# Shifting the overlaid buffers of a two-layer decoder kernel by 384 bytes per partition

## The chip, the cores and the metric

The kernel runs on one core of a Trainium2 chip. The metric is the device time of one launch in microseconds (us), as the median of three runs. All data are 32-bit floats. Matrix products are done in the fp32r form of TensorE.

## What is computed

The reference is a trunk of two layers on 512 tokens of 1024 channels:

```python
for l in range(DEPTH):                                   # DEPTH = 2
    h = h + hybrid_mixer(rms_norm(h, norm1_g[l]), ...)   # three attention branches, gates, output projection
    h = h + peer_ffn(rms_norm(h, norm2_g[l]), ...)       # 8 heads, top 16 of 16384 experts
return rms_norm(h, final_g)

# the end of hybrid_mixer
merged = (gates[:, :, 0] * (oa @ w_br_a) + gates[:, :, 1] * (ob @ w_br_b) + gates[:, :, 2] * (oc @ w_br_c))
return merged @ w_out

# peer_ffn, per chunk of tokens
act = jnp.einsum('thkd,td->thk', u[ids], xc)
w = g * jax.nn.gelu(act, approximate=False)
y = jnp.einsum('thk,thkd->td', w, v[ids])
```

## The kernel before, in words

**Weights.** Every weight is streamed from HBM in chunks of 128 partitions x 2048 floats (1 MB). SyncE's queue loads a chunk into `raw` (L379). ScalarE copies it to `hi` in the shorter fp32r form (L501), and VectorE writes `lo = raw - hi` (L836). All three have two buffers. Each mathematical product is three matmuls, written by one helper, `product` (L1322):

```python
pe.matmul(dst, a_[0], b_[0], start=first, stop=False)        # L1325  a_hi, b_hi
pe.matmul(dst, a_[0], b_[1], start=False, stop=False)        # L1326  a_hi, b_lo
return pe.matmul(dst, a_[1], b_[0], start=False, stop=last)  # L1327  a_lo, b_hi
```

The first operand of a matmul is the stationary one (128 columns, loaded into the array), the second is the moving one (streamed through it, up to 512 columns). The trace names the moving operand first: `bank<-oT_hi,hi` has `oT_hi` moving and `hi` stationary.

**Stages of a layer, in order of time.** (1) Projections and attention for three pairs of heads. ScalarE and VectorE write the attention output to `oT_hi` and `oT_lo`. (2) Merge: 24 steps M. A step makes the gate product (24 matmuls, `xT` moving, weights stationary, 512 columns) and the branch product (9 matmuls, `oT` moving, weights stationary, 512 columns); in the first four steps of a layer the gate products were done earlier, and the 36 branch matmuls stand by themselves. The merged result goes to `mg_hi` and `mg_lo`. (3) Output projection: 192 matmuls, here `mg` is stationary and the weight chunk moves, 512 columns. (4) Queries and key scores: `xT` moving. (5) U: 64 chunks of 48 matmuls, `xT` moving (352 of the 512 tokens), weights stationary; beside the first 14 the experts are chosen, and beside the next 30 TensorE makes small products of `onehot` tables, which give the gates per expert. (6) V: 64 chunks of 48 matmuls, the weights stationary, `w_hi`/`w_lo` (activation times gate) moving, 352 columns. The other 160 tokens do not go through TensorE in U and V: GpSimd gathers their expert rows by indirect DMA into `rows` (L490), and VectorE multiplies and adds them (L1202 to L1215).

In a V chunk the matmuls run in groups of six: three with `w_hi[:, s, 0]`/`w_lo[:, s, 0]` moving, then three with `w_hi[:, s, 1]`/`w_lo[:, s, 1]`, where `s` is the parity of the chunk.

**How the buffers lie.** SBUF tensors are laid out one after another, in the order of their declarations in `build` (L215 to L306). Sets that are never alive together share one place: `oT`, the attention buffers or the merge buffers, and, over the same bytes, the buffers of the expert stages. Starts in bytes per partition, worked out from the sizes:

| buffer | start before | modulo 1024 | start after | modulo 1024 |
|---|---|---|---|---|
| xT_hi, xT_lo | 32896, 49280 | 128 | same | 128 |
| raw, hi, lo (two each) | 65664 to 106624 | 128 | same | 128 |
| ident | 114816 | 128 | same | 128 |
| keysT | 122496 | 640 | same | 640 |
| oT_hi, oT_lo | 128768, 147200 | 768 | 129152, 147584 | 128 |
| proj | 165632 | 768 | 166016 | 128 |
| v_ab, kv, qT, kT, lg, pT | 180224 to 219136 | 0 | 180608 to 219520 | 384 |
| mg_hi, mg_lo, gates, acc, part, xs | 165632 to 206592 | 768 | 166016 to 206976 | 128 |
| act_s | 133376 | 256 | 133760 | 640 |
| qhT | 145664 | 256 | 146048 | 640 |
| gate_s, onehot, rows | 145664, 178432, 194816 | 256 | 146048, 178816, 195200 | 640 |
| gate_in, w_lo, act_in | 145664, 168192, 179456 | 256 | 146048, 168576, 179840 | 640 |
| w_hi, act_k | 173824, 185088 | 768 | 174208, 185472 | 128 |

A piece of a weight chunk or of `mg` (128 columns) is 512 bytes long, one of `xT`, `oT` 2048, one of `w_hi` 1408.

Of the kernel before, what the change touches and what calls it, by code (L numbers as in the profile page):

```python
# [28 lines left out]
P = 128  # L29
# [177 lines left out]
def build(nc, a, out):  # L207
# [4 lines left out]
    with ExitStack() as ctx:  # L212
        def sb(name, shape, dt=F32, to=ctx):
            return to.enter_context(nc.sbuf_tensor(name, shape, dt))
# [26 lines left out]
        ss, rms, rstd = sb("ss", [P, NT]), sb("rms", [P, NT]), sb("rstd", [P, NT])  # L241
        mx, nmx = sb("mx", [P, NU]), sb("nmx", [P, NU])
        den, esink, rden = sb("den", [P, NU]), sb("esink", [P, NU]), sb("rden", [P, NU])
        to_line = sb("to_line", [P, 8])


        mixer = ExitStack()
# [1561 lines left out]
```

## Time and profile before

| | |
|---|---|
| median of three runs | 3311.99 us (3311.56 to 3313.68) |
| the profiled execution | 3316.17 us, its span 3314.4 us |
| TensorE busy | 3269.3 us, 99% of the span |
| VectorE, ScalarE, GpSimd busy | 79%, 47%, 33% |
| DMA | 894.83 MB, mean 270 GB/s |
| mean granted TensorE clock | 0.998 |

A busy TensorE is not one at its peak: the records of successive matmuls overlap, so the pace is read from the distance of their starts.

### The profile page before, as it was taken

What the parts mean: (1) busy time and instruction counts of PE and PEld (TensorE: products, weight loads), DVE (VectorE), ACT (ScalarE), POOL (GpSimd) and SP (SyncE); (2) the same over time, 40 slices, a digit from 0 to 9 for tenths busy, and PEclk for the clock granted to TensorE, in tenths of its full rate; (3) what the DMA queues carried; (4) which work ended last, traced back from release to release, by engine and by line L of the source; (5) the groups of instructions that cost most, each with busy time, mean ns of one, the idle gap of its engine ahead of it and who ended that gap; (6) DMA issues with size and microseconds to landing.
All of it is one profiled execution on the core that took longest, in us unless ns stands there. A gap on an engine that the chain in (4) does not pass through costs nothing. (4 is left out here: it accounts for less than half of the span.)

```text
span 3314.4 us, 55810 instructions
## 1 busy us (share of the span) xinstructions
PE 3269.3 (99%) x19734; PEld 3039.2 (92%) x19734; DVE 2610.5 (79%) x4992; ACT 1554.9 (47%) x2368; POOL 1087.6 (33%) x711
## 2 busy tenths in 40 slices
PE   8999999999999999999999999999999999999998
PEld 7767878999999999999987678789999999999998
DVE  6555448999997899999855644399999978999897
ACT  5554332467774333333355543334677733333333
POOL 1000003423335555555300000134333345555552
PEclk9999999999999999999999999999999999999999
DMA  4113322479999999999721133224899999999996
GB/s 146 62 52 115 140 104 81 171 286 383 379 383 389 420 403 411 403 409 410 284 90 64 42 124 140 103 82 176 310 379 382 378 404 416 402 409 407 404 405 251
DMA packets 230935, 894.83 MB, mean 270 GB/s; under 512 B 22784, under 2 KB 67984, under 8 KB 182912
## 3 DMA queue, kind: packets, MB, share of 16 engines
q1 hardware_dynamic: 116944, 465.34, 36.7%
q0 software_dynamic: 93008, 337.91, 26.1%
q10 hardware_dynamic: 20832, 89.74, 6.7%
q8 instruction: 72, 1.18, 0.1%
q14 instruction: 79, 0.65, 0.1%
HBM read 801.42 MB, written 91.49 MB: 269 GB/s over the span
## 5 line engine op out<-in xcount | busy, mean ns | idle before, releaser
L836 DVE TENSOR_TENSOR lo<-raw,hi 128x2048 fp32r<-128x2048 f32 (+1 forms) x320 | 728.9, 2278 | 287.4 <-ACT hi L501 284.9
L1325 PE MATMUL bank<-xT_hi,hi 128*128 128x352 f32 (+1 forms) x2688 | 928.7, 346 | 1.9 <-DVE xT_lo L886 1.7
L1326 PE MATMUL bank<-xT_lo,hi 128*128 128x352 f32 (+1 forms) x2688 | 911.5, 339 | 0.0
L1327 PE MATMUL bank<-xT_hi,lo 128*128 128x352 f32 (+1 forms) x2688 | 911.3, 339 | 0.0
L501 ACT ACTIVATE hi<-raw 128x2048 fp32r<-128x2048 f32 (+1 forms) x338 | 643.9, 1905 | 375.9 <-PE bank L1327 338.2
L1325 PE MATMUL bank<-w_hi,hi 128*128 128x352 f32 x2048 | 661.1, 323 | 0.5 <-DVE w_lo L1243 0.5
L1327 PE MATMUL bank<-w_hi,lo 128*128 128x352 f32 x2048 | 661.5, 323 | 0.0
L1326 PE MATMUL bank<-w_lo,hi 128*128 128x352 f32 x2048 | 658.1, 321 | 0.0
L1325 PEld LDWEIGHTS bank<-xT_hi,hi 128*128 128x128 f32 x2688 | 506.5, 188 | 32.3 <-issue 5.6
L490 POOL DMA_INDIRECT rows<-in_v_rows,ids x256 | 415.8, 1624 | 350.5 <-DVE h L1215 276.1
L1327 PEld LDWEIGHTS bank<-xT_hi,lo 128*128 128x128 f32 x2688 | 505.7, 188 | 26.0
L1326 PEld LDWEIGHTS bank<-xT_lo,hi 128*128 128x128 f32 x2688 | 507.2, 189 | 23.1
L490 POOL DMA_INDIRECT rows<-in_u_rows,ids x256 | 325.3, 1271 | 394.0 <-DVE act_row L1204 309.8
L1327 PEld LDWEIGHTS bank<-w_hi,lo 128*128 128x128 f32 x2048 | 386.7, 189 | 0.0
L1325 PEld LDWEIGHTS bank<-w_hi,hi 128*128 128x128 f32 x2048 | 384.4, 188 | 1.6 <-issue 1.0
L1326 PEld LDWEIGHTS bank<-w_lo,hi 128*128 128x128 f32 x2048 | 385.8, 188 | 0.0
L1215 DVE SCALAR_TENSOR_TENSOR h<-rows,w_row,h 128x1024 f32<-128x1024 f32 x256 | 327.6, 1280 | 7.3 <-DVE h L1215 1.4
L1204 DVE CUSTOM_DVE_ANT_0 rows<-rows,x_row 128x1024 f32<-128x1024 f32 x256 | 301.1, 1220 | 12.6 <-DMA rows<-in_u_rows,ids 12.6
L791 ACT ACTIVATE w_hi<-act_in 128x704 fp32r<-128x704 f32 x120 | 95.3, 794 | 392.2 <-DVE act_in L1238 392.2
L706 ACT ACTIVATE act_s<-bank 128x352 f32<-128x352 f32 x124 | 57.6, 465 | 278.3 <-PE bank L1327 278.3
L1262 DVE TENSOR_SCALAR onehot<-iota_sb,idx1T,gT 128x128 f32<-128x128 f32 x704 | 185.8, 356 | 1.0 <-ACT gT L738 1.0
L1623 PE MATMUL bank<-onehot 128*128 128x128 f32 x1408 | 176.0, 275 | 0.0
(227 smaller groups left out, 4254.1 us busy)
## 6 DMA issues: line engine op xcount, KB each, us to landing
raw<-in_stream SPq DMA_DIRECT2D x352, 1024.0 KB, 6.6
gate_d<-gate_s ACTq DMA_DIRECT2D x22, 2048.0 KB, 11.9
act_d<-act_s ACTq DMA_DIRECT2D x120, 352.0 KB, 6.4
act_in<-act_d SPq DMA_DIRECT2D x120, 352.0 KB, 7.0
gate_in<-gate_d SPq DMA_DIRECT2D x96, 384.0 KB, 9.6
gate_in<-gate_d SPq DMA_DIRECT2D x32, 256.0 KB, 4.8
rows<-in_u_rows,ids POOLq DMA_INDIRECT x256, 10.0
rows<-in_v_rows,ids POOLq DMA_INDIRECT x256, 7.5
```

Source lines behind the costliest of these rows:

```text
L490: pool.indirect_dma_start(rows[:, N % NR], None, a["u_rows" if n < U_ROW_OPS else "v_rows"], bass.IndirectOffsetOnAxis(which, 0)).then_inc ...
L501: act.activation(hi[s][:, 0:n], raw[s][:, 0:n], ACT.Copy).then_inc(hi_done, 1)
L706: act.activation(dst[:, s, 1, 0:TU], ps[1][:, 0:TU], ACT.Gelu).then_inc(gelu1, 1)
L791: act.activation(w_hi[:, s], acts_of(k, s), ACT.Copy).then_inc(w_hi_done, 1)
L836: dve.tensor_tensor(lo[s][:, 0:n], raw[s][:, 0:n], hi[s][:, 0:n].bitcast(F32), ALU.subtract).then_inc(lo_done, 1)
L1204: last = dve.tensor_tensor_reduce(row, row, x_row[:], 1.0, 0.0, ALU.mult, ALU.add, act_row[:, k])
L1215: last = dve.scalar_tensor_tensor(out=h[:, ROWED], in0=row, scalar=w_row[:, k], in1=h[:, ROWED], op0=ALU.mult, op1=ALU.add)
L1262: last = dve.tensor_scalar(o[:, r, 0], iota[:], idx1T[:, t], gT[:, t], ALU.is_equal, ALU.mult)
L1325: pe.matmul(dst, a_[0], b_[0], start=first, stop=False)
L1326: pe.matmul(dst, a_[0], b_[1], start=False, stop=False)
L1327: return pe.matmul(dst, a_[1], b_[0], start=False, stop=last)
L1623: last = pe.matmul(ps[4 + slot][:, tile(r)], o[:, 1], o[:, 0], start=True, stop=True)
```

## The change

`to_line` is a tensor that nothing reads or writes. It stands last before the overlaid buffers and grows by 96 floats, 384 bytes. Everything declared before it keeps its place, everything after it (from `oT_hi` on) moves up by 384 bytes. The last buffer then ends at 227968 of 229344. No instruction is added, removed or moved on any engine.

```diff
@@ -241,7 +241,7 @@
         ss, rms, rstd = sb("ss", [P, NT]), sb("rms", [P, NT]), sb("rstd", [P, NT])
         mx, nmx = sb("mx", [P, NU]), sb("nmx", [P, NU])
         den, esink, rden = sb("den", [P, NU]), sb("esink", [P, NU]), sb("rden", [P, NU])
-        to_line = sb("to_line", [P, 8])
+        to_line = sb("to_line", [P, 8 + 96])
```

## Rows read from the trace of the kernel before

**Rows 1.** The page: engines, then 40 slices of the span in tenths.

```profile
PE 3269.3 (99%) x19734; PEld 3039.2 (92%) x19734; DVE 2610.5 (79%) x4992; ACT 1554.9 (47%) x2368; POOL 1087.6 (33%) x711
...
PEclk9999999999999999999999999999999999999999
DMA  4113322479999999999721133224899999999996
```

**Rows 2.** Timeline of PE, one merge step: start us, duration us, engine, line, operands.

```profile
332.94 0.40 PE L1325 MATMUL bank<-oT_hi,hi 128*128 128x512 f32 x1
...
335.04 0.39 PE L1325 MATMUL bank<-xT_hi,hi 128*128 128x512 f32 x1
...
336.42 0.39 PE L1325 MATMUL bank<-xT_hi,hi 128*128 128x512 f32 x1
...
340.50 0.40 PE L1325 MATMUL bank<-oT_hi,hi 128*128 128x512 f32 x1
```

**Rows 3.** Timeline of PE, output projection: its first matmul and what follows its last.

```profile
433.31 0.39 PE L1325 MATMUL bank<-hi,mg_hi 128*128 128x512 f32 x1
...
477.92 0.71 PE L1353 MATMUL bank<-ident_sb,xs 128*128 128x128 f32 x5
```

**Rows 4.** Groups by form, 295 to 433.3 us: count, busy us, mean ns, idle before.

```profile
L1326 PE MATMUL bank<-xT_lo,hi 128*128 128x512 f32 x145 | 56.6, 391 | 0.0
...
L1325 PE MATMUL bank<-oT_hi,hi 128*128 128x512 f32 x57 | 22.5, 395 | 0.0
```

**Rows 5.** Timeline of PE: starts of two successive chunks each, U then V.

```profile
624.50 0.33 PE L1325 MATMUL bank<-xT_hi,hi 128*128 128x352 f32 x1
...
632.24 0.33 PE L1325 MATMUL bank<-xT_hi,hi 128*128 128x352 f32 x1
...
1050.26 0.32 PE L1325 MATMUL bank<-xT_hi,hi 128*128 128x352 f32 x1
...
1057.94 0.32 PE L1325 MATMUL bank<-xT_hi,hi 128*128 128x352 f32 x1
...
2960.28 0.32 PE L1325 MATMUL bank<-w_hi,hi 128*128 128x352 f32 x1
...
2967.91 0.32 PE L1325 MATMUL bank<-w_hi,hi 128*128 128x352 f32 x1
...
3113.86 0.33 PE L1325 MATMUL bank<-w_hi,hi 128*128 128x352 f32 x1
...
3121.59 0.33 PE L1325 MATMUL bank<-w_hi,hi 128*128 128x352 f32 x1
```

**Rows 6.** Groups by form, whole span: plain fp32 matmuls of 128 columns.

```profile
L1623 PE MATMUL bank<-onehot 128*128 128x128 f32 x1408 | 176.0, 275 | 0.0
...
L1573 PE MATMUL bank<-keysT,qhT 128*128 x256 | 30.9, 275 | 0.0
```

**Rows 7.** Groups by form, whole span: VectorE tensor_tensor of three lengths.

```profile
L836 DVE TENSOR_TENSOR lo<-raw,hi 128x2048 fp32r<-128x2048 f32 x316 | 724.0, 2291 | 284.4 <-ACT hi L501 281.9
...
L1243 DVE TENSOR_TENSOR w_lo<-act_in,w_hi 128x704 fp32r<-128x704 f32 x120 | 106.1, 884 | 1.8 <-ACT w_hi L791 1.7
...
L1051 DVE TENSOR_TENSOR acc<-acc,part 128x512 f32<-128x512 f32 x32 | 22.1, 692 | 1.1
```

**Rows 8.** DMA queues, 700 to 1000 us: packets, MB, share of 16 engines.

```profile
q0 software_dynamic: 14194, 51.67, 45.6%
q1 hardware_dynamic: 4180, 30.44, 26.2%
q10 hardware_dynamic: 5616, 31.43, 25.8%
```

**Rows 9.** DMA in V, 1200 to 1600 us, and its issues.

```profile
DMA packets 53475, 162.56 MB, mean 406 GB/s; under 512 B 4649, under 2 KB 22953, under 8 KB 46806
...
raw<-in_stream SPq DMA_DIRECT2D x52, 1024.0 KB, 7.4
```

**Rows 10.** Waits, 1200 to 1600 us: total us, times, longest.

```profile
ACT hi L501 <- PE bank L1327: 87.7, 52, 1.7
```

**Rows 11.** DMA, 10 to 60 us: GB/s in 40 slices.

```profile
GB/s 410 385 363 254 3 52 197 419 170 0 0 203 419 229 26 223 433 157 0 0 0 0 13 242 419 184 7 0 0 0 52 288 433 66 0 52 295 433 59 0
```

## The prediction

> **What bounds the kernel now.** I read the page first. TensorE is busy for 99% of the span, and the granted clock is full (2.4 GHz) in all 40 slices; VectorE stands at 79% [rows 1]. So the time is the number of matmuls times their pace. The DMA digits are 9 through U and V, so transfers are the second candidate there. A busy TensorE does not tell its pace, so next I read the starts of matmuls in the timeline. In a merge step [rows 2] nine matmuls with `oT` moving start 233.3 ns apart ((335.04 - 332.94) / 9). The 24 with `xT` moving that follow begin at 230 ns (335.04 to 336.42 is six), and then run at 226.7 ns (336.42 to 340.50 is 18). Shape, weights and stage are the same, and none of them waited [rows 4]: idle before is 0.0 for both. In the output projection 192 matmuls take 477.92 - 433.31 = 44.61 us [rows 3], 232.3 ns each, again at 512 columns, now with the weights moving and `mg` stationary.
>
> **What the two kinds have in common.** The weight chunks and `xT` start 128 bytes beyond a multiple of 256. `oT` and `mg` start on a multiple of 256. A product of two operands with equal remainder modulo 256 settles at 226.7 ns. One of unequal remainder stays at 232 to 233 ns, whichever of the two is stationary. After the change `oT` and `mg` have the remainder 128 as well.
>
> **The sum, against the profiled execution (3316.17 us).**
> - Merge, steps 4 to 23. One step is 33 matmuls in 340.50 - 332.94 = 7.56 us [rows 2]. At 226.7 ns throughout it would be 7.48. That is 0.08 us, times 20 steps, times 2 layers: **3.2 us**. It counts the matmuls with `xT` that begin at 230 ns: I take them to be slow because they follow `oT`, so they settle too.
> - Merge, steps 0 to 3: 36 matmuls per layer by 6.6 ns, 0.24 us, twice: **0.5 us**. A wait breaks this run in two, and a matmul after a wait seems to need some others before it settles, so 0.4.
> - Output projection: 44.61 - 192 x 0.2267 = 1.08 us, twice: **2.2 us**.
> - Sum: 3.2 + 0.4 + 2.2 = **5.8 us**. All of it lies on the path, since TensorE waits for nothing there [rows 4]; ScalarE and VectorE wait for it. The bounds: nothing if the remainder is not the cause, 5.9 if every such matmul gets to 226.7.
>
> **What I cost at nothing, and why.**
> - V. A piece of `w_hi` is 1408 bytes, 5.5 times 256, so in each group of six matmuls three have `w` on remainder 0 and three on remainder 128. The change swaps the two. Groups alternate without a break, so it is the same sequence, begun one place later. The price per chunk is not a constant, though: 7.63 us at 2960 us, 7.73 at 3113 [rows 5]. In U, where all operands have remainder 128, it is 7.74 at 624 and 7.68 at 1050. So at 352 columns there are paces 53 ns per chunk apart (7.63, 7.68, 7.73) that hold for many chunks, in both kinds of operands. The kernel may settle otherwise in V after the change. With 128 chunks of V, most near 7.68, each at most 0.053 away, that is at most 6.8 us either way. I take 0 and keep both ends.
> - The plain fp32 matmuls (attention, transposes, scores, gates per expert). `onehot` has both operands on remainder 0, `keysT`/`qhT` has 128 against 0: both 275 ns [rows 6]. Nothing.
> - VectorE and ScalarE. `acc` and `part` lie on remainder 0 (692 ns for 512), `act_in` too (884 for 704), `raw`, `hi`, `lo` on 128 (2291 for 2048) [rows 7]. (884 - 692) / 192 = 1.00 ns per element and (2291 - 884) / 1344 = 1.05: one line, so the remainder costs nothing I can see. The bound from the pair is 0.05 ns per element; VectorE has room for it outside V, and in V on half its work it would be hidden too.
> - DMA. The moved buffers `rows`, `gate_in`, `act_in` (written) and `act_s`, `gate_s` (read) go from remainder 0 to 128. From 700 to 1000 us queue q1 writes `raw` alone, with remainder 128: 26.2% of 16 x 300 us for 30.44 MB is 41.3 us per MB. q0 writes `rows`, with remainder 0: 42.4. q10 reads `act_s` and `gate_s` with remainder 0: 39.4 [rows 8]. So writing at 128 is not dearer than at 0. Reads of SBUF at 128 are not shown. The bounds are 0 and 42.4 / 39.4 = 1.076 times.
>
> The Trainium skill, page "DMA: Bandwidth & Descriptors", section "How a descriptor splits into AXI transactions", speaks against this change: a descriptor that does not start on a multiple of 256 bytes begins with a transaction from the boundary below, so bytes before its start are fetched and not used. An estimate from its figures (4 beats of 32 bytes more per packet, 16 engines at 27.2 GB/s, 1028 packets in a V chunk) is 0.30 us of DMA time per chunk. The trace does not agree for writes, where `raw` is no dearer than `rows` [rows 8]; no run yet shows it for reads.
>
> **The rivals.**
> 1. *The remainder is not the cause.* `oT` and `mg` could be slow for another reason, such as a place high in memory, or the order in which banks are filled. For it: `w_hi` and `w_lo` lie high as well and with half of them on the unequal remainder, V is not slower than U [rows 5]. Against it: `mg` as stationary and `oT` as moving share little else, and `xT` in the same step settles within six matmuls. Time: 3312.0.
> 2. *V settles on another pace.* If all of V goes to 7.63, 5.8 + 6.8 = 12.6 us are gained, 3299.4. If all goes to 7.73 the gain is lost: 3312 - 5.8 + 6.8 = 3313. Each end is unlikely, parts of the way are not, since the pace changes within V of one layer.
> 3. *Slower: the transfers of V become the bound.* Place: the 128 chunks of V. A chunk moves 162.56 MB / 52 = 3.13 MB in 7.68 us [rows 9]. The fastest slice in the trace is 433 GB/s [rows 11], at which it takes 7.22 us, so there are 0.46 us, 6%, in hand. ScalarE's copy to `hi` never waits for a load but for TensorE, by 1.7 us each time (87.7 / 52) [rows 10]; that is the second reserve. If moved transfers cost 7.6% more, a chunk needs 7.77 us, 0.09 more than TensorE; the reserve of 1.7 us is used up after some 19 chunks of a layer, and then 45 x 0.09 x 2 = 8 us are lost. With the 5.8 gained: 3314. If U, whose DMA digits are 9 as well, pays as much for its 50 busiest chunks, another 8: 3322. It decides from 6% on. Against it: [rows 8].
>
> By the Trainium skill's estimate of 0.30 us a chunk needs 7.52 us, still below 7.68: by that rule alone the time would not change.
>
> **How the numbers follow.** The likeliest case is the sum: 3311.99 - 5.8 = **3306.2 us**. (The profiled execution lies 4.2 above the median; the difference is made on either.) A measurement of this kernel can tell about 0.2% from no change, 6.6 us, so this forecast is "within 0.2%", by less than a microsecond. Chances of the cases: the sum with V about as before (within 3 us) 0.55; the sum with V settling more than that faster 0.15, more slowly 0.10; the remainder not the cause 0.13; transfers 0.07. The first case lies on either side of the line at 3305.4: I give 0.22 of its 0.55 to faster. **Faster** by over 0.2% is 0.22 + 0.15 + a little from a V that settles with rival 1: 0.38. **Slower** by over 0.2% (above 3318.6) needs the transfers, or V at its slow end with no gain: 0.07. **Same** is 0.55. The range goes from 3299.4 (all of V at its fast pace) to 3314 (V at its slow pace, or the first step of rival 3).
>
> **What would show it in the profile after.** Merge steps of 7.48 us with `oT` starting 226.7 ns apart; an output projection of 43.5 us; V and U chunks still 7.63, 7.68 or 7.73, in whatever mixture; per-MB costs of the DMA queues as before; ScalarE's `hi` still waiting for TensorE by about 1.7 us in V. The prediction is wrong if `oT` stays at 233 ns (rival 1), if the chunks of V change by more than 53 ns, or if a load releases `hi`.

## The result and the profile after

The kernel became slower, not a little faster: the median is 3320.58 us (3318.37 to 3323.99, 13 runs) against 3313.80 us (3311.29 to 3317.83, 13 runs) for the kernel before, measured again beside it. The two medians are 0.2% apart; the estimated ratio is 1.0015, with a 95% interval of 1.0008 to 1.0022. The forecast was 3306.2 us, with a range that ended at 3314.

The profiled execution's span is 3318.7 us, 4.3 more than before. The row of the page that answers to [rows 1]:

```profile
PE 3267.1 (98%) x19734; PEld 3039.5 (92%) x19734; DVE 2610.7 (79%) x4992; ACT 1554.6 (47%) x2368; POOL 1112.1 (34%) x711
```

TensorE is busy for 2.2 us less, in a span that is longer. So it does its work faster and stands still more. First the part that got faster, the timeline of PE over one merge step and the ends of the output projection (start us, duration us):

```profile
332.19 0.39 PE L1325 MATMUL bank<-oT_hi,hi 128*128 128x512 f32 x1
...
334.23 0.39 PE L1325 MATMUL bank<-xT_hi,hi 128*128 128x512 f32 x1
...
339.67 0.39 PE L1325 MATMUL bank<-oT_hi,hi 128*128 128x512 f32 x1
...
431.47 0.39 PE L1325 MATMUL bank<-hi,mg_hi 128*128 128x512 f32 x1
...
475.00 0.71 PE L1353 MATMUL bank<-ident_sb,xs 128*128 128x128 f32 x5
```

Against [rows 2]: the nine matmuls with `oT` start (334.23 - 332.19) / 9 = 226.7 ns apart, where they had taken 233.3. The step takes 339.67 - 332.19 = 7.48 us, where it had taken 7.56. Against [rows 3]: the output projection takes 43.53 us, where it had taken 44.61. The forecast had 226.7 ns, 7.48 us and 43.5 us.

Then the part that got slower. These are waits from 1200 to 1600 us, in V of the first layer (who <- for whom, total us, times, longest):

```profile
ACT hi L501 <- PE bank L1327: 58.5, 37, 2.5
...
ACT hi L501 <- DMA raw<-in_stream: 29.9, 14, 2.7
...
PEld bank L1325 <- DVE w_lo L1243: 2.8, 6, 0.8
```

In [rows 10] ScalarE's copy to `hi` had waited for TensorE 52 times out of 52. Now it waits for TensorE 37 times and 14 times for the load of `raw`, which had never been late. The DMA view of the same stretch (GB/s in 40 slices of 10 us), before, and then after, with its sum:

```profile
GB/s 415 327 418 419 415 419 417 410 409 417 389 414 420 384 401 420 407 412 414 388 389 415 421 408 417 410 391 415 394 416 404 415 406 397 415 414 412 407 381 415
...
GB/s 403 373 408 404 403 406 402 405 402 404 407 403 402 406 404 401 409 401 403 407 402 404 404 406 401 405 405 404 404 402 405 404 406 402 405 404 404 404 401 403
DMA packets 53165, 161.28 MB, mean 403 GB/s; under 512 B 4619, under 2 KB 22881, under 8 KB 46574
```

Before, the mean was 406 GB/s [rows 9], with slices up to 421 and dips between them, as of queues that sometimes ran dry. Now all slices but one (373) lie between 401 and 409, as of queues that never do. Transfers have become the bound of V in stretches.

What the waits cost TensorE can be read from the distances of its matmuls' starts. In V before, one gap stands out in each layer, 0.4 us in the first chunk. After, layer 0 has seven more, 4.7 us together, and layer 1 two more, of 1.0 and 2.0 us. Right behind these two the granted clock falls to the lower level, 1.2 GHz, for 3.4 us, and the chunk it falls in takes 9.31 us, 1.6 more than 7.68. The waits in V of layer 1 (2815 to 3295 us), and the window of the low clock (from:to us, length, busy us and count for PE, PEld, DVE, ACT, POOL, then clock, DMA share, GB/s):

```profile
ACT hi L501 <- DMA raw<-in_stream: 18.0, 8, 3.8
PEld bank L1325 <- DVE w_lo L1243: 3.5, 3, 2.1
```

```profile
3180.40:3183.80 3.40, 3.40 (x14) 3.40 (x13) 3.40 (x3) 0.30 (x1) 3.40 (x1) 0.50 0.99 388
```

So gaps make up 7.7 us and the clock 1.6 of the 10.0 us that V lost in the two layers.

The times of the stages, from the starts of their first and last matmuls, in us:

| stage | before | after | difference |
|---|---|---|---|
| merge and output projection, both layers | 2 x 205.3 | 2 x 202.5 | -5.6 |
| V, layer 0 | 492.0 | 497.7 | +5.6 |
| V, layer 1 | 492.9 | 497.3 | +4.3 |
| U, layer 0 | 572.6 | 574.6 | +2.0 |
| U, layer 1 | 572.3 | 572.4 | +0.2 |
| attention and all else | | | -2.2, so that the sum is the span's +4.3 |

Of the last row, 1.6 us lie between the last V matmul of layer 0 and the first merge matmul of layer 1 (271.2 us before, 269.6 after). In the trace before, the granted clock was at 1.2 GHz there for 3.4 us, after V had ended and TensorE had been idle for up to 2.2 us at a time; in the trace after it stayed at 2.4 GHz:

```profile
1658.90:1662.30 3.40, 3.40 (x19) 3.40 (x18) 1.17 (x3) 0.70 (x3) 0.00 (x0) 0.51 0.00 0
```

The traces of runs 2 and 5 to 9 below show such a fall at that place, those of runs 1, 3 and 10 do not. It follows no buffer that was moved, so these 1.6 us are no gain of the change.

### The profile page after: what moved, and what is told of

It is laid out like the page before. It is cut to its first block and busy times, and to the rows that moved or that the text cites. A ratio compares the mean times of both kernels' runs of the same rounds, so it can differ in the third digit from the quotient of the medians.

```text
span 3318.7 us, 55810 instructions
## 1 busy us (share of the span) xinstructions
PE 3267.1 (98%) x19734; PEld 3039.5 (92%) x19734; DVE 2610.7 (79%) x4992; ACT 1554.6 (47%) x2368; POOL 1112.1 (34%) x711
## 5 line engine op out<-in xcount | busy, mean ns | idle before, releaser
L490 POOL DMA_INDIRECT rows<-in_v_rows,ids x256 | 440.6, 1721 | 339.5 <-DVE h L1215 265.0
```

The source lines that it names most:

```text
L490: pool.indirect_dma_start(rows[:, N % NR], None, a["u_rows" if n < U_ROW_OPS else "v_rows"], bass.IndirectOffsetOnAxis(which, 0)).then_inc ...
```

## The experiments

The theory after the result: (a) a matmul with 512 columns is slowed when its stationary and its moving operand have unequal remainders modulo 256 bytes, and that gain is real; (b) a DMA packet whose SBUF side starts off a multiple of 256 costs its engine a fixed extra time, and this carries the transfers of V past what TensorE hides. The rivals: the loss in V is chance between executions; it comes from `w_hi` and `w_lo` being read at other remainders; it goes with bytes, not packets. All verdicts are against the kernel before, whose median beside these runs was 3315 us. A trace shows one execution of each run; the waits and stage times below are those of that one.

**1. Only the mixing buffers moved.** The change, and a filler that puts the expert buffers back on their old remainder:

```diff
-        to_line = sb("to_line", [P, 8])
+        to_line = sb("to_line", [P, 8 + 96])
...
+        to_old = sb("to_old", [P, 160])
         idx1T, idx2T = sb("idx1T", [P, TD]), sb("idx2T", [P, TD])
```

> The change for oT, mg and the attention buffers only; a filler of 640 bytes in front of idx1T puts every buffer of the expert stages back on its old remainder (modulo 1024). My theory (the gain of 5.8 us in merge and output projection is real, and the moved expert buffers cost about 10 us in V): 5 to 6 us below the kernel before, V spans of about 492.5 us as before, no wait of hi for raw in V. Rival (the loss in V comes from moving the mixing buffers, or is chance between executions): V stays at about 497.5 us and the time within 2 us of the changed kernel.

Measured: 3308.97 us (11 runs) against 3314.78, ratio 0.9982 (0.9973 to 0.9991). This beats both kernels. Its output projection, in the timeline of PE:

```profile
432.01 0.39 PE L1326 MATMUL bank<-hi,mg_hi 128*128 128x512 f32 x1
...
475.54 0.71 PE L1354 MATMUL bank<-ident_sb,xs 128*128 128x128 f32 x5
```

That is 43.53 us. From 1200 to 1600 us `hi` waits for TensorE again and for no load:

```profile
ACT hi L502 <- PE bank L1328: 86.3, 51, 1.8
```

**2. The converse.** Only the expert buffers moved:

```diff
+        to_new = sb("to_new", [P, 96])
         idx1T, idx2T = sb("idx1T", [P, TD]), sb("idx2T", [P, TD])
```

> The converse: oT, mg and the attention buffers stay where they were, the buffers of the expert stages move by the same 384 bytes. My theory: merge steps of 7.56 us and an output projection of 44.6 us as before, V spans of about 497.5 us with waits for raw, and a time of 3313.8 + 10 to 12, some 3324 to 3326 us. Rival (chance, or the mixing buffers): about 3314.

Measured: 3325.62 us (6 runs), ratio 1.0033 (1.0021 to 1.0045). V takes 497.0 and 496.1 us. From 1200 to 1600 us:

```profile
ACT hi L502 <- PE bank L1328: 55.8, 34, 2.7
...
ACT hi L502 <- DMA raw<-in_stream: 31.5, 16, 2.8
```

So the two halves add up: about -6 by themselves for the mixing buffers (run 1), +11 for the expert buffers (run 2), and +5 to +7 together. The loss is not chance, and it comes from the second half.

**3. Only w_lo and w_hi moved**, on top of run 1:

```diff
+        pad_a = sb("pad_a", [P, 32], to=weigh)
         w_lo, w_hi = sb("w_lo", [P, 2, 2, TU], F32R, weigh), sb("w_hi", [P, 2, 2, TU], F32R, weigh)
+        pad_b = sb("pad_b", [P, 32], to=weigh)
```

> As e1_mix_only, but w_lo and w_hi alone lie 128 bytes further (fillers of 128 bytes before and behind them), so that only the moving operands of V change their remainder and no buffer that a DMA touches does. If the loss in V comes from the transfers: as e1_mix_only, within 2 us. If it comes from the matmuls reading w_hi and w_lo in the other order of remainders: V longer by some 5 us in each layer, 3318 us.

Measured: 3308.01 us (11 runs), ratio 0.9981 (0.9972 to 0.9990), as in run 1. The matmuls of V do not mind which half of `w` has which remainder. What is left of the second half are the buffers that a DMA touches.

**4. The price by itself.** A probe that only transfers:

```diff
+    for width, q in ((256, 8), (704, 3), (1024, 2), (2048, 1)):
+        for bufs in (even, odd):
+            phase(bufs, width, q, False)
+    for width, q in ((704, 3), (2048, 1)):
+        for bufs in (even, odd):
+            phase(bufs, width, q, True)
```

> No part of the model is computed: the output is zeros, and the kernel is twelve phases of 24 loads of about 1 MB from SyncE's queue, four in flight. Packets of 1024, 2816, 4096 and 8192 bytes are written into SBUF at remainder 0 (even) and at 128 (odd), then packets of 2816 and 8192 bytes are read from SBUF at either. Theory (a start off a multiple of 256 costs each packet a fixed extra of about 5 ns on its DMA engine): 1024-byte phases some 10% longer at 128, 2816-byte ones 4%, 4096-byte ones 3%, 8192-byte ones 1.5%. Rival (the remainder does not matter to a transfer): each pair of phases within 1%.

Measured: in time-stretches inside each of the twelve phases (from:to us, length, two idle engines, clock, DMA share, GB/s), in the order of the code: writes of 1024, 2816, 4096, 8192 bytes, then reads of 2816 and 8192, each at remainder 0 and then at 128:

```profile
30.00:80.00 50.00, 0.00 (x0) 0.00 (x0) 1.00 1.09 386
95.00:155.00 60.00, 0.00 (x0) 0.00 (x0) 1.00 1.10 348
168.00:222.00 54.00, 0.00 (x0) 0.00 (x0) 1.00 1.03 412
234.00:290.00 56.00, 0.00 (x0) 0.00 (x0) 1.00 1.03 398
302.00:354.00 52.00, 0.00 (x0) 0.00 (x0) 1.00 1.02 420
366.00:420.00 54.00, 0.00 (x0) 0.00 (x0) 1.00 1.03 410
432.00:482.00 50.00, 0.00 (x0) 0.00 (x0) 1.00 1.01 427
493.00:544.00 51.00, 0.00 (x0) 0.00 (x0) 1.00 1.01 423
556.00:608.00 52.00, 0.00 (x0) 0.00 (x0) 1.00 1.04 415
620.00:675.00 55.00, 0.00 (x0) 0.00 (x0) 1.00 1.03 392
688.00:738.00 50.00, 0.00 (x0) 0.00 (x0) 1.00 1.01 427
748.00:798.00 50.00, 0.00 (x0) 0.00 (x0) 1.00 1.01 420
```

A packet of B bytes takes 16 x B / rate on its engine. 1024 bytes: 42.4 ns at 386 GB/s, 47.1 at 348, so 4.6 more (11%). 2816 bytes: 109.4 and 113.2, 3.8 more (3.5%). 4096: 156.0 and 159.8, 3.8 more. 8192: 307.0 and 309.9, 2.9 more. Reads: 108.6 and 114.9, 6.4 more; 307.0 and 312.1, 5.1 more. So the price is close to fixed per packet, 3 to 5 ns for a write and 5 to 6 for a read. (The expectations of runs 5 to 7 use the mean duration of the packets' records instead, which grew by 5.5, 4 and 3.4 ns at 1024, 4096 and 2816 bytes.) The probe's loads go through SyncE's queue; the price on GpSimd's queue, which fills `rows`, is taken to be the same.

For V: 17,067 packets of 4096 bytes (`rows`) lie between 1200 and 1600 us in the trace after, some 330 per chunk. `gate_in` brings 352 packets of 1024 bytes per chunk and `act_in` 128 of 2816. On one of 16 engines that is 330 / 16 x 3.8 + 352 / 16 x 4.6 + 128 / 16 x 3.8 = 0.078 + 0.101 + 0.030 = 0.21 us more per chunk. At the flat 404 GB/s a chunk's 3.13 MB takes 7.74 us, so before it needed an estimated 7.53. The probe's own packet times, summed over the four kinds of packets of a chunk, give 7.72 and 7.50, without 89 packets of 4 bytes that a chunk has as well. TensorE's 7.68 lies between the two.

**5 to 7. One buffer back at a time.** On the changed kernel, fillers of 128 bytes put one buffer back on remainder 0. The edit for `gate_in`; `act_in` has the same around it, `rows` only the one in front:

```diff
+        pad_a = sb("pad_a", [P, 32], to=weigh)
         gate_in = sb("gate_in", [P, 2, SLICES, I_PER_LOAD, SLICE], to=weigh)
+        pad_b = sb("pad_b", [P, 32], to=weigh)
```

> The changed kernel with gate_in alone put back on remainder 0 (fillers of 128 bytes before and behind it). The probe showed 5.5 ns more for a 1024-byte packet, so a V chunk's 352 such packets need 352 / 16 x 5.5 = 0.12 us less on each DMA engine: 7.74 - 0.12 = 7.62 us, under the 7.68 of TensorE. Theory (extra time per packet, V is held up only above 7.68): no or nearly no wait of hi for raw, time 3310, nearly all of the loss gone. Rival (it is the number of bytes that matters, not of packets): gate_in is a tenth of the bytes, so a tenth of the 10 us comes back, 3319.

> The changed kernel with rows alone put back on remainder 0. 333 packets of 4096 bytes per chunk at 4 ns: 0.08 us less, 7.66 us per chunk, just under TensorE's 7.68. Theory per packet: most of the loss gone, 3311. Rival by bytes: rows is 43% of the bytes, 4 us back, 3316.

> The changed kernel with act_in alone put back on remainder 0. 128 packets of 2816 bytes per chunk at 3.4 ns: 0.03 us less, 7.71 us per chunk, still above TensorE's 7.68. Theory: waits for raw remain, some 4 us of 10 come back, 3316.

Measured:

| run | us (11 runs each) | ratio to before | waits of `hi` for `raw` in V |
|---|---|---|---|
| `gate_in` back | 3312.42 | 0.9993 (0.9984 to 1.0002) | none |
| `rows` back | 3312.16 | 0.9995 (0.9986 to 1.0004) | none |
| `act_in` back | 3314.37 | 0.9998 (0.9989 to 1.0007) | 7, in layer 1 |

The row of the last one, 2815 to 3295 us:

```profile
ACT hi L503 <- DMA raw<-in_stream: 14.7, 7, 2.7
```

`gate_in` is a tenth of V's bytes and a third of its packets. Putting it back alone removes every wait for a load from the trace, as putting back `rows` does, which is 43% of the bytes. That speaks for the price per packet together with a threshold: with the probe's prices a chunk needs 7.74 - 0.10 = 7.64 us with `gate_in` back, 7.66 with `rows`, 7.71 with `act_in`. What it has to be held against is TensorE's pace in that execution, which is not always 7.68. The matmuls that start from 1200 to 1600 us in runs 5, 6 and 7:

```profile
1200.00:1600.00 400.00, 400.00 (x2518) 1.00 1.03 410
```

```profile
1200.00:1600.00 400.00, 400.00 (x2519) 1.00 1.03 409
```

```profile
1200.00:1600.00 400.00, 400.00 (x2484) 1.00 1.03 404
```

That is a pace of 7.63 us per chunk in the first two and 7.73 in the third. At 7.63, transfers of 7.64 and 7.66 fall behind by 0.5 to 1.6 us over some 55 chunks, which the 1.7 us that `hi` has in hand [rows 10] cover. At 7.73, transfers of 7.71 keep up, and layer 0 of run 7 has no wait for a load; its seven waits are in layer 1, where TensorE ran mostly at 7.63.

The times came out 2.4 and 1.2 us above the first two expectations, and 1.6 below the third. The first two traces are of short executions (3309.25 and 3306.47 us, where the medians are 3312.42 and 3312.16), so whether the longer ones waited for loads is not shown. Run 8, measured beside them, ended some 4 us below both; the intervals of the ratios still overlap. So one buffer put back brings some 8 of the 11.6 us by which the changed kernel lies above run 1, and whether the rest is real, and what it is, stays open.

**8. Every large transfer at remainder 0.** Run 1, and fillers around `raw`, which had lain at 128 in all kernels:

```diff
+        pad_a = sb("pad_a", [P, 32])
         raw = [sb(f"raw{s}", [P, CW]) for s in range(2)]
+        pad_b = sb("pad_b", [P, 32])
```

> As e1_mix_only, and raw too on remainder 0 (fillers before and behind it; hi, lo and xT keep 128), so that no large transfer starts off a multiple of 256. A chunk's transfers become 128 / 16 x 5 = 0.04 us shorter still. Theory: TensorE bounds V already in e1_mix_only, so the time is the same as there within 2 us, 3309, with DMA packets of 8192 bytes some 1 to 2% shorter. Rival (V in e1_mix_only is still held by transfers here and there): 2 us or more faster.

Measured: 3308.43 us (10 runs), ratio 0.9980 (0.9971 to 0.9990): the same as run 1. Its packets of 8192 bytes took 315.2 ns on average in V of layer 1 and 315.9 in run 1, 0.2% less and not 1 to 2%, so that part of the expectation missed. Once the transfers fit under TensorE, making them fit better buys nothing.

**9 and 10. Which remainder the matmuls want.** Run 1 with `oT` and `mg` at 64 and at 192 bytes beyond a multiple of 256. The edit of the first; the second has 112 and 144:

```diff
-        to_line = sb("to_line", [P, 8 + 96])
+        to_line = sb("to_line", [P, 8 + 80])
...
-        to_old = sb("to_old", [P, 160])
+        to_old = sb("to_old", [P, 176])
```

> As e1_mix_only, but oT, mg and the attention buffers begin 64 bytes beyond a multiple of 256, while xT, hi and lo stay at 128; the expert buffers are as before. If the pace asks for equal remainders modulo 256: output projection about 232 ns per matmul, 44.4 us. If it is enough to be off the multiple of 256: 226.7 ns, 43.3 us.

> The same with 192 bytes beyond a multiple of 256. Equal remainders needed: 232 ns. Off the multiple of 256 is enough: 226.7 ns. If only the distance to the partner counts, as e9_mix_at_64 or its mirror.

Measured: the output projection of the first, then of the second, first matmul and end:

```profile
433.25 0.40 PE L1326 MATMUL bank<-hi,mg_hi 128*128 128x512 f32 x1
...
478.06 0.71 PE L1354 MATMUL bank<-ident_sb,xs 128*128 128x128 f32 x5
```

```profile
435.16 0.39 PE L1326 MATMUL bank<-hi,mg_hi 128*128 128x512 f32 x1
...
479.95 0.71 PE L1354 MATMUL bank<-ident_sb,xs 128*128 128x128 f32 x5
```

44.81 and 44.79 us, 233.4 and 233.3 ns each, and the same in the second layer. (Each kernel was executed once, in 3319.61 and 3314.73 us, against 3315.53 for the kernel before.) Of 0, 64, 128 and 192 only 128, the remainder of the weights, gives 226.7. So it is not enough to be off the multiple. That the operands must be equal is the simplest reading and not more: the weights lay at 128 in every run, so no pair that is equal at another remainder was tried, and with the pieces of `mg` and of the weights 512 bytes long, a rule modulo 512 would give the same results.

**11. Which remainder a transfer wants.** The probe again, with 1024-byte packets written at eight offsets:

```diff
+    for shift in (0, 8, 16, 24, 32, 40, 48, 56):
+        phase(even, 256, 8, False, shift)
```

> No part of the model is computed. Eight phases of 24 loads of 1 MB in packets of 1024 bytes, written at 0, 32, 64, 96, 128, 160, 192 and 224 bytes beyond a multiple of 256. A fixed price for any start off the multiple: seven phases alike, some 10% longer than the first. A price that grows with the offset: longer from phase to phase. A price by multiples of 64 or 128: a mixture.

Measured: stretches in the first, the second, the fifth and the eighth phase:

```profile
30.00:80.00 50.00, 0.00 (x0) 0.00 (x0) 1.00 1.09 386
95.00:155.00 60.00, 0.00 (x0) 0.00 (x0) 1.00 1.09 348
...
320.00:380.00 60.00, 0.00 (x0) 0.00 (x0) 1.00 1.10 348
...
545.00:600.00 55.00, 0.00 (x0) 0.00 (x0) 1.00 1.09 348
```

All seven shifted phases give 348 GB/s. The price is the same for 32 bytes as for 224, so it is not the number of bytes before the start that is paid, but the fact of not starting on the multiple.

## Why the prediction was wrong

**What held.** The sum for merge and output projection was 5.8 us and measures 5.6: a merge step of 7.48 us and an output projection of 43.53, as stated. That the start of `oT` and `mg` is the cause (against rival 1, which has a place high in memory or the order of banks) is shown by runs 1, 2, 9 and 10; that it is equality modulo 256 is not shown in full (run 10). That `w_hi` and `w_lo` may swap their remainders for nothing is shown by run 3.

**The step that failed** is "What I cost at nothing", its point on DMA: "So writing at 128 is not dearer than at 0." It is, by 3 to 5 ns per packet. The reading of [rows 8] compared cost per byte between queues with packets of different sizes: `raw` moves in 8192-byte packets and `rows` in 4096-byte ones, and what is fixed per packet counts half as much per byte on `raw`. That covered the very thing that was looked for, also something fixed per packet. The right comparison would have held the packet size fixed, and no buffer of this kernel offered it: the trace before does not show the price.

The Trainium skill, page "DMA: Bandwidth & Descriptors", section "How a descriptor splits into AXI transactions", had been set aside because of that row. The probe agrees with it that a start off the multiple costs, and for 128 bytes its 4 beats (4.7 ns, an estimate from its figures) are close to what run 4 measures at 1024 bytes, 4.6; at 4096 and 8192 bytes it measures less, 3.8 and 2.9. It does not agree in how the cost goes with the offset: by that section 32 bytes would cost one beat and 224 bytes seven, and run 11 shows one price for all; there the measurement decides. The estimate in the prediction, 0.30 us per chunk, was made for all packets; the runs give 0.21 for those that moved.

**The second failure** is in rival 3: it named the right place, the right mechanism and the right sign, and gave it 0.07. It put the reserve at 6%, from "the fastest slice in the trace", 433 GB/s. In that slice [rows 11], at the start of the kernel, only 8192-byte packets move. A third of V's packets have 1024 bytes, and the probe moves those at 386 GB/s even at remainder 0. V's mixture needs 7.53 us per chunk by the account of run 4, so the reserve was 0.15 us, 2%. With a reserve of 2% in place of 6%, and a known cost of 0.21 us, the same working gives V a pace of 7.74 us. The 1.7 us that ScalarE's copy has in hand [rows 10] last for 28 chunks of a layer at 0.06 us each, and 36 x 0.06 x 2 = 4.3 us are lost, where the profile shows 10.0. So the right price alone would have made the forecast "no change", not "slower". Two more things were missing. TensorE was taken at 7.68 us throughout; in the trace after it runs at 7.63 in 33 of V's chunks, where transfers fall behind by 0.11. And a wait can cost more than itself: the low clock behind the waits of layer 1 took 1.6 us. V's 10.0 and U's 2.2 us outweigh the 5.6 gained.

**Not foreseen at all**: U of layer 0 is 2.0 us longer. Each of its chunks beside the `onehot` products takes 10.41 us from start to start where it took 10.35, and the last ones 7.73 where they took 7.68, without a wait; the first ones are faster, 7.68 for 7.73. Runs 2 and 5 show the same. Layer 1 of the changed kernel itself, and run 7, in which all buffers that U uses lie as in the change, show 10.36 and 7.68, so the addresses alone do not decide it. (U of layer 0 in run 7 is still longer, 575.8 us, by one wait of 1.9 us and 3.4 us at 1.2 GHz behind it.) What selects the pace is open.

## What to carry to other kernels

Keep the SBUF side of every sizeable transfer on a multiple of 256 bytes, small packets first; and give the two operands of fp32r matmuls with 512 columns the same remainder modulo 256, of which 128 with 128 is the pair that was measured. Here the two wishes concern different buffers and can be met together with fillers of 384 and 640 bytes, as in run 1: 3309 us. When judging how much room a saturated transfer stage has, take the rate of a stage with the same packet sizes, not the best rate in the trace.

## What was not expected of the hardware

- TensorE's pace depends on where its operands lie: with the weights at remainder 128 modulo 256, 226.7 ns for 512 columns with `mg` at 128 as well, 232.3 with it at 0, 233.4 and 233.3 at 64 and 192. At 352 columns no loss was seen: half of V's matmuls have `w` at 0, and V's chunks take 7.63 to 7.73 us as U's do, where all operands have 128; run 3 swaps the halves for nothing. The Trainium skill, page "TensorE: Matmul & The Clock Gate", section "Step-by-step: what each phase is for", says that loading the next weights does not steal SBUF read bandwidth from the running matmul, since the two have separate read ports. No run here shows whether the 6 ns are lost in these reads; the mechanism was not tried.
- The pace of V has three values, 7.63, 7.68 and 7.73 us per chunk, which hold for many chunks and differ between executions of kernels that have the same addresses there. Runs 1, 9 and 10 differ only in the mixing buffers, yet V of layer 0 took 492.3, 495.1 and 488.8 us in them. The matmuls that start from 1200 to 1600 us, in runs 9 and 10:

```profile
1200.00:1600.00 400.00, 400.00 (x2484) 1.00 1.02 404
```

```profile
1200.00:1600.00 400.00, 400.00 (x2519) 1.00 1.03 409
```

  TensorE is never idle in either. This is 1.4% of V's pace. V of one layer differs by up to 6.3 us with it, so it can account for a good part of the scatter of 3303 to 3313 us between the executions of run 1; what sets it was not tried.
